# Feed-forwards with 512-column products over a rounded and a low half, summed at the drain

## The reference

```python
# four times, D = 1024, D_FF = 2816: ffn1 and ffn2 of two layers
x = x + 0.5 * swiglu(rmsnorm(x, ffn1_norm[layer]), ffn1_w_gu[layer], ffn1_w_down[layer])
def swiglu(h, w_gu, w_down):
    gate, up = jnp.split(h @ w_gu, 2, axis=-1)
    return (jax.nn.silu(gate) * up) @ w_down
...
# once, D_FF_2 = 4096: up, squared relu, down
```

## Time and profile before

| | before |
|---|---|
| median of 3 runs | 1651.73 us (1643.67 to 1655.06) |
| span of the profiled execution | 1644.7 us |
| TensorE matmuls busy | 1575.0 us, 96%, 15413 records |
| VectorE busy | 1066.6 us, 65% |
| ScalarE busy | 732.9 us, 45% |
| GpSimd busy | 69.7 us, 4% |
| DMA | 243.23 MB, 148 GB/s over the span |

### The profile page before, as it was taken

The page is one execution under the profiler, slowest core; times in us unless marked ns, Lnnn a source line. Parts: engine busy times, 40 slices in busy tenths (PEclk is TensorE's granted clock), DMA queues, the critical chain, the costliest instruction groups (busy, mean ns, idle before and its releaser), DMA issues.

```text
span 1644.7 us, 35602 instructions
## 1 busy us (share of the span) xinstructions
PE 1575.0 (96%) x15413; PEld 1514.6 (92%) x15413; DVE 1066.6 (65%) x1277; ACT 732.9 (45%) x814; POOL 69.7 (4%) x51
## 2 busy tenths in 40 slices
PE   7999999999999999999999999999979899999998
PEld 7999999888999999999979999988967778999997
DVE  5776497665866466663867665567676654877446
ACT  5433355443543354333555333455563323465333
POOL 2000000000100010000101000120000000100000
PEclk9999999998999999999999999999999998999999
DMA  8665544203565555655425655554300011555552
GB/s 268 186 197 194 191 154 163 70 3 103 180 195 189 204 180 179 188 189 186 155 81 168 187 180 192 186 175 131 105 2 2 3 53 52 180 182 202 186 199 77
DMA packets 155063, 243.23 MB, mean 148 GB/s; under 512 B 9283, under 2 KB 106174, under 8 KB 154814
## 3 DMA queue, kind: packets, MB, share of 16 engines
q1 hardware_dynamic: 154510, 240.63, 45.1%
q10 hardware_dynamic: 432, 0.79, 0.2%
HBM read 240.34 MB, written 1.05 MB: 147 GB/s over the span
## 4 chain that ended last, share of the span: by engine, by line
PE 87%; DVE 6%; ACT 3%; issue 1%; DMA 1%; POOL 0%; SPq 0%; ACTq 0%; DVEq 0%
PE dense_ps L2383 24%; PE dense_ps L2384 24%; PE dense_ps L2385 24%; PE mixer_ps L449 3%; PE dense_ps L449 2%; DVE w_lo L2753 1%; PE mixer_ps L1643 1%; PE mixer_ps L1081 1%; ACT ly_r L495 0%; PE mixer_ps L1072 0%; DVE xT L2871 0%; PE mixer_ps L1649 0%; DMA raw<-in_ffn_w_gu 0%; ACT score_b L1111 0%; ACT w_hi L2580 0%
## 5 line engine op out<-in xcount | busy, mean ns | idle before, releaser
L2753 DVE TENSOR_TENSOR w_lo<-raw,w_hi 128x2048 fp32r<-128x2048 f32 x225 | 523.2, 2336 | 241.7 <-ACT w_hi L2580 240.8
L2383 PE MATMUL dense_ps<-h_hi,w_hi 128*128 128x256 f32 x2368 | 667.6, 282 | 11.7 <-DVE h_lo L2828 8.1
L2384 PE MATMUL dense_ps<-h_lo,w_hi 128*128 128x256 f32 x2368 | 661.2, 279 | 0.0
L2385 PE MATMUL dense_ps<-h_hi,w_lo 128*128 128x256 f32 x2368 | 661.1, 279 | 0.0
L2580 ACT ACTIVATE w_hi<-raw 128x2048 fp32r<-128x2048 f32 x225 | 428.4, 1913 | 334.1 <-DMA raw<-in_ffn_w_down 116.7
L2383 PEld LDWEIGHTS dense_ps<-h_hi,w_hi 128*128 128x128 f32 x2368 | 450.8, 190 | 17.9 <-issue 17.3
L2384 PEld LDWEIGHTS dense_ps<-h_lo,w_hi 128*128 128x128 f32 x2368 | 447.4, 189 | 0.9 <-issue 0.5
L2385 PEld LDWEIGHTS dense_ps<-h_hi,w_lo 128*128 128x128 f32 x2368 | 447.4, 189 | 0.0
L2383 PE MATMUL dense_ps<-g_hi,w_hi 128*128 128x256 f32 x960 | 266.7, 278 | 0.0
L2384 PE MATMUL dense_ps<-g_lo,w_hi 128*128 128x256 f32 x960 | 266.7, 278 | 0.0
L2385 PE MATMUL dense_ps<-g_hi,w_lo 128*128 128x256 f32 x960 | 266.7, 278 | 0.0
(11 more groups left out here) (537 smaller groups left out, 1819.9 us busy)
## 6 DMA issues: line engine op xcount, KB each, us to landing
raw<-in_ffn_w_gu SPq DMA_DIRECT2D x176, 512.0 KB, 4.7
raw<-in_ffn_w_down SPq DMA_DIRECT2D x88, 512.0 KB, 4.2
raw<-in_w_ff SPq DMA_DIRECT2D x64, 512.0 KB, 4.2
raw<-in_w_in SPq DMA_DIRECT2D x36, 512.0 KB, 4.4
raw<-in_a_w_in SPq DMA_DIRECT2D x32, 512.0 KB, 4.4
raw<-in_a_w_out SPq DMA_DIRECT2D x8, 512.0 KB, 4.2
raw<-in_b_w_in SPq DMA_DIRECT2D x8, 512.0 KB, 4.2
raw<-in_b_w_out SPq DMA_DIRECT2D x8, 512.0 KB, 4.0
```

Of the source, the lines that this page charges most:

```text
L2383: pe.matmul(o, hi, mh, start=start, stop=False)
L2384: pe.matmul(o, hi, ml, start=False, stop=False)
L2385: return pe.matmul(o, lo, mh, start=False, stop=stop)
L2753: dve.tensor_tensor(w_lo[:, p % SLOTS, :], raw[:, p % SLOTS, :], w_hi[:, p % SLOTS, :].bitcast(F32), ALU.subtract).then_inc(lo_ready, 1)
```

## The change

It touches the feed-forwards only; the mixers keep `three`, their hi and low operands now lie in one tensor of two halves (`h_both`, `g_both` and so on).

- **The product** (`apart`): one matmul of 512 columns, w_hi on (h_hi, h_lo), fills one PSUM bank: hi·hi in its first 256 columns, hi·low in the other 256. A second matmul of 256 columns, w_lo on h_hi, adds to the first 256. Two matmuls and two weight loads stand for three and three. The sum of the two halves of the bank is left to the drain.
- **Up** (`run_ring`): a tile now takes a whole bank, so a piece is two tiles over all eight k (a piece of gate, then one of up), and four pairs of banks, D_ps and M_ps, are used in turn.
- **Drain of up**: after each piece ScalarE copies the second halves to SBUF (`side2`), VectorE adds the first halves to them (`summed`), then scales, multiplies as before; rounding to g_hi moves from VectorE to ScalarE. In ffn4 the relu no longer reads PSUM but the sum.
- **Down** (`run_half`): the output is computed in two halves of four tiles, each over all k, a half in four banks; the pieces are loaded to suit (512 columns of four k). The residual adds the two halves of each bank one after the other (`residual_apart`), the first half of the output midway through the down projection.
- **Start of a stage**: the first two pieces are taken for k 0 to 3 both, then for k 4 to 7.

```diff
-JOBS = [("gu0", "narrow", 11), ("down0", "wide", 11), ("a_in", "narrow", 8), ("a_out", "wide", 4),
-        ("gu1", "narrow", 11), ("down1", "wide", 11), ("gu2", "narrow", 11), ("down2", "wide", 11),
-        ("b_in", "narrow", 3), ("b_out", "wide", 4), ("gu3", "narrow", 11), ("down3", "wide", 11),
+JOBS = [("gu0", "ring", 22), ("down0", "half", 11), ("a_in", "narrow", 8), ("a_out", "wide", 4),
+        ("gu1", "ring", 22), ("down1", "half", 11), ("gu2", "ring", 22), ("down2", "half", 11),
+        ("b_in", "narrow", 3), ("b_out", "wide", 4), ("gu3", "ring", 22), ("down3", "half", 11),
         ("in2", "narrow", 9), ("up_attn", "wide", 2), ("up_rwkv", "wide", 2), ("out2", "wide", 4),
...
-            def three(o, hi, lo, mh, ml, start, stop):
-                pe.matmul(o, hi, mh, start=start, stop=False)
-                pe.matmul(o, hi, ml, start=False, stop=False)
-                return pe.matmul(o, lo, mh, start=False, stop=stop)
+            def three(o, hi, lo, both, start, stop):
+                pe.matmul(o, hi, both[:, 0, :], start=start, stop=False)
+                pe.matmul(o, hi, both[:, 1, :], start=False, stop=False)
+                return pe.matmul(o, lo, both[:, 0, :], start=False, stop=stop)
+            def apart(bank, hi, lo, both, start, stop):
+                pe.matmul(bank.rearrange("p (s t) -> p s t", s=2), hi, both, start=start, stop=False)
+                return pe.matmul(bank[:, 0:T], lo, both[:, 0, :], start=False, stop=stop)
+            def run_ring(job):
+                p0, f0, n = PIECE_OF[job], FILL_OF[job], COUNT_OF[job]
+                stage = stage_of[job]
+                h0 = h_before(stage)
+                groups = ring(stage)
+                def products(j, turn, ks, fresh=False):
+                    p = p0 + j
+                    ps, b = groups[j % 4]
+                    if ks[0] == 0:
+                        if j >= 4:
+                            pe.wait_ge(dense_drained, 2 + f0 + j - 4 + 1 + 4 * turn)
+                        pe.wait_ge(lo_ready, p + 1 + 4 * turn)
+                    for k in ks:
+                        if fresh and k % 2 == 0:
+                            pe.wait_ge(h_ready, h0 + k // 2 + 1)
+                        for i in range(2):
+                            w0 = 2 * P * k + P * i
+                            last = apart(ps[:, b + i, :], w_hi[:, p % SLOTS, w0:w0 + P], w_lo[:, p % SLOTS, w0:w0 + P],
+                                         h_both[:, :, k, :], start=k == 0, stop=k == KD - 1)
+                    if ks[-1] == KD - 1:
+                        last.then_inc(piece_used, 1)
...
+                    before = 2 + FILL_OF[BEFORE[stage]]
+                    pe.wait_ge(dense_drained, before + 1)
+                    products(0, 0, range(4), True)
+                    if stage == "ffn1":
+                        pe.wait_ge(dense_drained, before + 2)
+                    products(1, 0, range(4))
+                    products(0, 0, range(4, 8), True)
+                    products(1, 0, range(4, 8))
+                    pe.wait_ge(dense_drained, before + 2)
+                norm(stage)
+                products(2, 0, range(8))
+                pe.wait_ge(rstd_ready, NORM[stage] + 1)
+                products(3, 0, range(8))
...
+            def run_half(job, moving, ready, between=None, midway=lambda: None):
+                p0, f0, n = PIECE_OF[job], FILL_OF[job], COUNT_OF[job]
+                nk = 2 * n
+                def product(u, nt):
+                    e, k = divmod(u, nk)
+                    p = p0 + u // 4
+                    w0 = 512 * (u % 4) + P * nt
+                    return apart(half_banks(job, e)[:, nt, :], w_hi[:, p % SLOTS, w0:w0 + P],
+                                 w_lo[:, p % SLOTS, w0:w0 + P], moving[:, :, k, :], start=k == 0, stop=k == nk - 1)
+                for u in range(2 * nk - 4):
+                    e, k = divmod(u, nk)
+                    if k == 0:
+                        pe.wait_ge(dense_drained, 2 + f0 - 2 + 2 * e)
...
+                    if u % 4 == 0:
+                        pe.wait_ge(lo_ready, p0 + u // 4 + 1)
+                    if e == 0 and k % 2 == 0:
+                        pe.wait_ge(g_ready, ready + k // 2 + 1)
+                    for nt in range(4):
+                        last = product(u, nt)
+                    if u % 4 == 3:
+                        last.then_inc(piece_used, 1)
+                    elif u == nk - 1:
+                        last.then_inc(half_filled, 1)
...
+                pe.wait_ge(lo_ready, p0 + n)
+                for nt in range(4):
+                    for u in range(2 * nk - 4, 2 * nk):
+                        last = product(u, nt)
+                    if nt == 1:
+                        last.then_inc(half_filled, 1)
+                last.then_inc(piece_used, 1)
...
+                    def side(j, jq):
+                        ps, b = groups[jq]
+                        act.wait_ge(piece_used, p0 + j + 1)
+                        act.activation(side2[:, jq % 2, :, :], ps[:, b:b + 2, T:2 * T], ACT.Copy).then_inc(side_kept, 1)
+                    def gated_(c, q, t=0, at_=0, lead=False):
+                        side(2 * c, 2 * q)
+                        if not lead:
+                            split_hi(t, at_)
+                        act.wait_ge(gate_scaled, c0 + c + 1)
                         act.activation(act2[:, q, :, :], act2[:, q, :, :], ACT.Silu).then_inc(act_ready, 1)
+                        side(2 * c + 1, 2 * q + 1)
+                        split_hi(t, at_ + 1 - lead)
+                        act.wait_ge(g_full, c0 + c + 1)
+                        act.activation(g_hi[:, bass.ds(2 * c, 2), :], full2[:, q, :, :], ACT.Copy).then_inc(g_rounded, 1)
+                    def squared(j):
+                        side(j, j % 4)
+                        if j:
+                            splits(1)
+                        act.wait_ge(dense_drained, 2 + f0 + j + 1)
+                        act.activation(act2[:, j % 2, :, :], act2[:, j % 2, :, :], ACT.Relu).then_inc(gate_scaled, 1)
+                        act.wait_ge(gate_scaled, c0 + j + 1)
+                        act.activation(act2[:, j % 2, :, :], act2[:, j % 2, :, :], ACT.Square).then_inc(act_ready, 1)
+                        act.wait_ge(g_full, c0 + j + 1)
+                        act.activation(g_hi[:, 2 * j:2 * j + 2, :], full2[:, j % 2, :, :], ACT.Copy).then_inc(g_rounded, 1)
...
+            def residual_apart(job, scale):
+                f0, p0, n = FILL_OF[job], PIECE_OF[job], COUNT_OF[job]
+                after = next_stage(stage_of[job])
+                def added(e, a, b):
+                    acc, x_ = half_banks(job, e), xT[:, 4 * e + a:4 * e + b, :]
+                    for side in range(2):
+                        last = dve.scalar_tensor_tensor(out=x_, in0=acc[:, a:b, T * side:T * side + T], scalar=scale,
+                                                        in1=x_, op0=ALU.mult, op1=ALU.add)
+                        if not side:
+                            link(last)
+                    return last
+                splits_to(p0 + (n + 1) // 2 + 2)
+                wait_half(dve, job, 0)
+                added(0, 0, 4).then_inc(dense_drained, 1)
+                splits(1)
+                if after in LATE_SCALE:
+                    before_norm(after, 0)
+                splits_to(p0 + n + 2)
+                dve.wait_ge(half_filled, HALF_OF[job] + (2 if n % 2 else 1))
+                added(1, 0, 2)
+                wait_half(dve, job, 1)
+                added(1, 2, 4).then_inc(dense_drained, 1)
...
+                    def summed(j, jq, out_):
+                        ps, b = groups[jq]
+                        dve.wait_ge(side_kept, SIDE_OF[up] + j + 1)
+                        dve.tensor_tensor(out_, ps[:, b:b + 2, 0:T], side2[:, jq % 2, :, :],
+                                          ALU.add).then_inc(dense_drained, 1)
+                    def rest_of(c, q):
+                        dve.wait_ge(g_rounded, c0 + c + 1)
                         k = bass.ds(2 * c, 2)
-                        split_act(full2[:, q, :, :], g_hi[:, k, :], g_lo[:, k, :]).then_inc(g_ready, 1)
+                        dve.tensor_tensor(g_lo[:, k, :], full2[:, q, :, :], g_hi[:, k, :].bitcast(F32),
+                                          ALU.subtract).then_inc(g_ready, 1)
+                    def gated_(c, q, t=0, at_=0, lead=False):
+                        summed(2 * c, 2 * q, act2[:, q, :, :])
+                        if lead:
+                            dve.wait_ge(rstd_ready, NORM[s] + 1)
+                        else:
+                            rest_of(c - 1, 1 - q)
+                        dve.wait_ge(dense_drained, 2 + f0 + 2 * c + 1)
+                        dve.tensor_tensor(act2[:, q, :, :], act2[:, q, :, :], by_rms(2), ALU.mult).then_inc(gate_scaled, 1)
+                        if not lead:
+                            split_lo(t, at_)
```

(16 more changed lines are left out.)

409 lines of the change are left out of this document (234 added, 175 removed).

## The result

The changed kernel takes 1671.94 us in the median (1668.01 to 1673.00) against 1647.70 for the kernel before beside it: a ratio of 1.0177, 95% interval 1.0113 to 1.0241. In a later run it was 1670.59 against 1638.50, 1.0204 (1.0170 to 1.0238). So the change makes the kernel 1.8 to 2% slower. The forecast was 1655 us, some 3 us over the median of the kernel before, with the likeliest case between 1% less and 1% more; what came is a clear loss, near the upper end of the range. The profiled executions are 1644.7 and 1671.0 us long: 26.3 us are to be found.

What follows compares the result with a forecast made beforehand. TensorE, busy 96% of the span, was taken to bound the kernel. Terms of +2, +7.5 and -1.7 gave +7.8 on 1644.7, about 1652.5; 2.5 added for spread made 1655 us, range 1605 to 1675.

Steps and rivals of the forecast that it cites:

- Term 1: Feed-forwards: a pair takes 346 ns where triples took 340 or 353; +9.4 and -7.4 us, together +2 us.
- The load-bound rival: Feed-forwards: weight loads bind the triple, so the pair takes 328 ns and the kernel 1611 us; chance 0.25.
- Term 2: ff1: ScalarE and VectorE need 6.0 us a turn against TensorE's 5.5 a piece, so TensorE waits; +7.5 us.
- the wait of 0.8 us at the first piece: ff1, after four pieces: TensorE waits 0.8 us for the low part of piece 4.
- Term 3: Stage starts after a down projection: three TensorE waits for h_lo go, -1.7 us; other starts unchanged.
- starts that follow a mixer's output projection: Stages behind a mixer's output projection: TensorE waits as long as before, no change in time.
- mixer_a's start: Before mixer_a: last squares, norm and scaling stand in a row as before, so nothing gained or lost.
- At nothing: Gated drains, gated stage starts, PSUM, weight refills, down's loads and SyncE's issues: no cost expected.
- the slower cadence everywhere: All feed-forwards: matmuls of 239 and 118 ns, pair 357 ns, kernel 1678 or 1680 us; chance 0.15.

Runs made afterwards that it cites:

- the cut pair: The changed kernel with each 512-column matmul cut into two of 256 with a load each, everything else as changed: 1649.61 us, 1.0006 of the kernel before.

## Why the pair takes 353 ns

First a stream of TensorE alone, ScalarE and VectorE idle, with triples, pairs, and the wide matmul by itself, with its columns contiguous or in two runs.

```
triple: hi x h_hi, hi x h_lo, lo x h_hi  (256 columns each)
pair:   hi x (h_hi | h_lo)  (512 columns), lo x h_hi  (256)
```

> A stream of TensorE alone, with the other engines idle: 17 sections of 96 blocks, each of one form, with a pause between them. Sections: triple (three loads, three times 256 columns), pair (one load and 512 columns in two runs of 256 that lie 8 KB apart, one load and 256 columns), pair_near (the 512 columns contiguous), the 512 columns alone in both layouts, three times 256 columns into two halves of a bank, and 256 columns alone with the same and with new weights. The output is not the reference's: nothing but these matmuls is computed. Theory A (columns bind, 0.46 ns each, a load costs nothing): 256 columns 113 to 118 ns, 512 columns 227 to 235 ns, triple 340 to 353, pair 340 to 353, both forms alike. Theory B (a start of a record costs some ns beside the columns, so the wide one is cheaper than two): 512 alone 216 to 230 ns, pair 328 to 346, below the triple by 7 to 12 ns. Theory C (the two runs of columns cost): the contiguous pair is 5 to 13 ns below the pair. Theory D (the slow and the fast cadence come from traffic of the other engines): all triples here at 340; if the cadence is TensorE's own, triples at both 340 and 353 may be seen.

Steps from start to start, in the steady part of each section: triples 360 ns (three of 120), pairs 353 (347 in one section of four), with contiguous columns 353 as well, the wide matmul alone 227, 256 columns alone 120. So the two runs cost nothing, and the pair carries 7 ns over 227 + 120. On the load the stream says little: the sections of 256 columns with new and with the same weights both step by 120, but the trace has a load for each matmul in either. That the load is not what costs shows in the kernels, where three loads a block go at 340 and two at 353. But the triple of this stream is slower than the kernels' by 20 ns, and the order of pair and triple is turned round. Theory D, other engines' traffic, fell. The same in the order of a ring piece, with groups of wide ahead of narrow ones:

```
g16: 16 x (hi x (h_hi | h_lo)), then 16 x (lo x h_hi)
```

> TensorE alone again, now with the kernel's own order of a ring piece (two outputs by eight k, start flag on the first k alone), 96 blocks a section. Sections: triple into one half of a bank; pair; the cut pair; pairs grouped so that 2, 4, 8 or 16 wide matmuls stand before as many narrow ones; wide alone; 256 columns alone, new and same weights; then triple, pair, grouped and cut pair again behind 7, 8 or 9 unrounded matmuls. The output is not the reference's. The first such stream had triples at 361 ns, pairs at 355, wide alone 228, 256 columns alone 120. Theory A (a change between the two widths costs some 7 ns each time, since wide alone is 228 and not 235): groups of 16 at 228 + 120 = 348 or less, near 341 if the narrow ones fall to 113, groups of 2 halfway. Theory B (the step is set by something else, as the cadence of the stream): all groupings at 353 to 355. On the cadence: if the start flag on every block made 120 ns there, the triples come to 340 here; if it is what runs ahead of the section, only those behind unrounded matmuls do; if neither, all stay at 360.

Triples 360 again (behind unrounded matmuls too), pairs 347, groups of 2 at 348, of 4 at 351, of 8 at 349, of 16 at 348, counted over whole pieces. (The expectation for the third stream has 341 for the last; that is a misreading.) So in this stream grouping gains nothing over the fast pair. In the kernel, where the pair is at 353, the ring piece (the down projection likewise, by fours):

```diff
-                        pe.wait_ge(lo_ready, p + 1 + 4 * turn)
+                        pe.wait_ge(hi_ready, p + 1 + 4 * turn)
...
-                        for i in range(2):
-                            last = apart(ps[:, b + i, :], w_hi[...], w_lo[...], h_both[:, :, k, :], ...)
+                        for i in range(2):
+                            pe.matmul(ps[:, b + i, :].rearrange("p (s t) -> p s t", s=2), w_hi[...], h_both[:, :, k, :], ...)
+                    if ks[0] == 0:
+                        pe.wait_ge(lo_ready, p + 1 + 4 * turn)
+                    for k in ks:
+                        for i in range(2):
+                            last = pe.matmul(ps[:, b + i, 0:T], w_lo[...], h_both[:, 0, k, :], ...)
```

> The changed kernel with the order of the pairs changed and nothing else: in a ring piece the sixteen wide matmuls come first and the sixteen narrow ones behind them (four and four in a down projection), and the wait for the low part stands before the narrow ones, so the wide ones wait for the rounded weights alone. Theory A (alternating widths costs 7 to 13 ns a pair): 2624 pairs by 7 to 12 ns are 18 to 31 us, and 4 us of waits for low parts go too: 1640 to 1650 us. Theory B (353 ns is what the columns cost in this cadence): only the waits go, 5 to 6 us: 1665 to 1667 us.

1658.08 us against 1641.30, 1.0093 (1.0055 to 1.0132): between the theories. Steady pairs are at 346.7 ns in all feed-forwards but ff1, 6.6 ns less, 17 us by 2624. ff1 gives its 1.7 of them back: its turn of 5.88 us still binds, and TensorE idles 2.4 us at the start of ff2 now. The waits for w_lo at the starts became waits of 0.4 to 0.8 us for h_both. So in the kernel the order of the widths is worth 6.6 ns a pair. What sets the step, then? Busy neighbours or a loop of TensorE's program could:

> TensorE in the order of a ring piece, as in the second stream, with triples and pairs beside: nothing; ScalarE copying 512 columns again and again; VectorE subtracting 512 columns again and again; both; DMA loads; all three; then the same out of a loop of TensorE's program, and over one piece of weights alone. The output is not the reference's. The second stream, TensorE alone, had triples at 360 ns, pairs at 347 and pairs grouped by sixteen at 341; the kernels have triples at 340 or 353, pairs at 353, grouped ones at 347. Theory A (other engines' work sets the cadence): with some of them triples go to 340 or 353 and pairs to 353, and the section says which engine. Theory B (the loop or the fetch of instructions sets it): only the looped sections go to 340. Theory C (neither): all sections read 360 and 347, and what sets the cadence in the kernels stays open.

```
triple, pair, each with: nothing | ScalarE | VectorE | both | loads | all | a loop | a loop and all | one piece
```

All triples 360 ns, pairs 347 (three sections of ten) or 353 without any pattern: theory C. What was left was where the operands lie. w_hi starts at byte 16512 of a partition and w_lo at 49280, both multiples of 128, in the kernels as in the streams. h_both starts at 122688 in the kernels, 64 beyond a multiple of 128 (g_both too), and at 90240 in the streams, which is a multiple.

> TensorE alone in the order of a ring piece once more, to find what sets the step of a 256-column matmul: 120 ns in the three streams before, 113 or 118 in the kernels. The moving operand lies first where it lay in those streams, then at the place that h_both has in the kernel, and at places 32, 64, 512 and 1024 bytes off that; then with VectorE draining each filled pair of banks and TensorE waiting for it as in the ring; then with a moving operand of zeros. The output is not the reference's. Theory A (the operand's place): triples at 340 or 353 in some of the placed sections and not in others. Theory B (waits and drains between the pieces): only the drained sections change. Theory C (the data): only the zeros change. Theory D: all stay at 360 and 347 to 354, and the cause stays open.

```
h at byte 90240 | 122688 | 141152 | 159616 | 178496 | 199488: 0, 64, 96, 0, 64, 64 beyond a multiple of 128
```

Theory A. The windows of six sections (us; PE busy and count; granted clock), triple and pair by turns with the operand 64, 96 and 0 bytes beyond a multiple of 128:

```profile
110.00:138.00 28.00, 28.00 (x249) 1.00 0.00 1
142.00:172.00 30.00, 30.00 (x172) 1.00 0.00 1
176.00:206.00 30.00, 30.00 (x256) 1.00 0.00 1
212.00:242.00 30.00, 30.00 (x175) 1.00 0.00 1
245.00:275.00 30.00, 30.00 (x253) 1.00 0.00 1
280.00:310.00 30.00, 30.00 (x171) 1.00 0.00 1
```

A window counts one or two records that began ahead of it. At the kernels' place 28 us hold 247 matmuls, 113.3 ns each and 340 a triple, and 30 us 85 pairs, 353: the numbers of the two kernels, with no other engine at work. At 96 it is 355 and 347, at 0 360 and 353. (The last of the six places, at 64 as well, has 353 for both.) With VectorE draining the banks, or zeros for data, triples at 0 stayed at 360.

> TensorE alone: triples and pairs, 96 blocks a section, with the weights (one piece) at four places and the moving operand at four, each 0, 32, 64 or 96 bytes beyond a multiple of 2048. The output is not the reference's. Theory A (the place of the moving operand alone): the same four numbers come back for each place of the weights; the stream before had the operand at 0 modulo 128: triple 360, pair 347 or 354; at 64: triple 340 or 353, pair 354; at 96: triple 355, pair 347. Theory B (the distance between weights and operand): the numbers move along with the difference of the two. Theory C (neither, luck of a section's start): no pattern.

```
for each place of the weights (0, 32, 64, 96) and of h (0, 32, 64, 96): 96 triples, 96 pairs
```

Theory B, the distance between weights and operand. Ordered by distance (h less weights, modulo 128), four sections of each, ns per block in the steady part of the section:

| distance | triple | pair |
|---|---|---|
| 0 | 360, 360, 360, 360 | 353, 353, 353, 353 |
| 32 | 350, 350, 350, 352 | 347, 347, 347, 347 |
| 64 | 353, 353, 340, 353 | 353, 353, 353, 353 |
| 96 | 360, 355, 355, 355 | 350, 353, 353, 347 |

Two of the windows behind it, triples at distance 64 with the weights at 64 (340 ns) and at distance 32:

```profile
597.00:625.00 28.00, 28.00 (x250) 1.00 0.00 1
...
806.00:834.00 28.00, 28.00 (x242) 1.00 0.01 1
```

At 64 the triple has two steps, 340 and 353, the fast and the slow cadence of the earlier trace rows. Which one a section falls into, the streams don't say. Nor does the distance fix every pair: at 0 the first stream has 347 in one section of four, the second in all, the third in three of ten. Only 32 and 64 gave the same number each time for widths by turns, 347 and 353.

Now the same in the kernels: some unused bytes ahead of the operand, no instruction changed. Distance 32 for the changed kernel, with the changed kernel itself beside it:

```diff
+    fixed.at += 96
     h_at = fixed.at
```

> The changed kernel with 96 unused bytes ahead of h_both, so the moving operands lie 32 bytes beyond a multiple of 128, as far from the weights as in the four sections of the crossed stream where a pair took 347 ns (triples 350 to 353 there). If the distance sets the step in the kernel: pairs 347, 2624 by 6.7 ns are 17 us less than the changed kernel, triples of the mixers, some 980, at 350 for 346 are 4 us more: 1656 to 1660 us. If only the triple's step follows the place and the pair stays at 353: 1671 to 1676 us.

> The changed kernel itself, on the same chip as the one with the operand moved by 96 bytes: 1671 us within 4, 1.3 to 2.0% over the kernel before.

1657.66 us, 1.0123 (1.0089 to 1.0156), the changed kernel beside it 1670.59, 1.0204 (1.0170 to 1.0238): 12.9 us less, where 13 were worked out. In the profiled executions ffn0 to ffn3 gain 14.4 us and mixer_a loses 3.5; ffn4 gains only 1.6, since ff1 still takes 94.8 us: its pieces come every 5.88 us as before, where 16 pairs are 5.55. L2440 (the wide matmul of this file) has 462 records in 160 us, 346 ns a pair:

```profile
620.00:780.00 160.00, 160.00 (x462) 86.53 (x462) 1.00 0.58 192
900.00:1040.00 140.00, 140.00 (x405) 75.83 (x404) 1.00 0.58 188
```

Distance 96 and distance 0 (`fixed.at += 32` and `+= 64`):

> The changed kernel with 32 unused bytes ahead of h_both, so h_both, g_both and the mixers' operands behind them lie 32 bytes further; no instruction is changed. If the place sets the step as in the last stream (pair 347 for 354 ns), 2624 pairs by 6.7 ns are 17 us less, and the triples of the mixers, some 980, cost up to 15 ns more each for those that were at 340: 1655 to 1668 us. If the place does not matter in the kernel: 1671 us within 3.

> The changed kernel with 64 unused bytes ahead of h_both. If the place sets the step: pairs at 347 to 354, triples of the mixers at 360, so the time from 10 us under to 10 us over 1671 us. If not: 1671 us within 3.

1675.73 us, 1.0208 (1.0180 to 1.0235): pairs stay at 353, a miss of what I expected of 96, where the crossed stream has 347 once in four. And 1681.79 us, 1.0244 (1.0210 to 1.0278), 1 us over what I allowed for, with pairs at 353 as in the changed kernel; what is lost stands in the mixers, 7 us of it in mixer_a, where triples go at 360. Last the kernel before, with `fixed.at += 64` ahead of h_hi:

> The kernel before with 64 unused bytes ahead of h_hi and no instruction changed. If the place sets the step (triple 360 ns there, 340 or 353 now): 1568 triples by 20 ns, 1056 by 7 and some 980 of the mixers by 7 to 20 are 45 to 58 us more: 1695 to 1708 us. If not: 1650 us within 3.

1689.86 us against 1641.56, 1.0293 (1.0265 to 1.0320): 48 us for 64 unused bytes, as many more as expected (45 to 58), though from a lower start than the 1650 that I had counted from. The windows of its L2384 (the h_hi line):

```profile
620.00:780.00 160.00, 125.54 (x443) 84.98 (x443) 1.00 0.58 183
900.00:1040.00 140.00, 108.95 (x384) 73.77 (x384) 1.00 0.57 180
```

443 triples in 160 us are 361 ns, and from start to start it is 360 in all of them. So the place moves the step in both kernels. With the operand at distance 0 the change as it stands would have made the kernel a little faster (1681.79 against 1689.86, ratios 1.0244 and 1.0293 on one chip; the intervals just overlap).

## Why the prediction was wrong, point by point

**Term 1, the pair: the step that failed.** Counts, cover and the level of the fast and slow triple were right; the price of the pair was 346 ns and is 353, in all 2624: the term was +2 us and measured +20. The error has two parts. The wide matmul steps by 235 ns when a narrow one follows, not by 233, and the narrow one behind it by 118, not 113. I had priced the two apart, from neighbours of their own kind, and added the narrow one at the fast step. With neighbours of their own kind, sixteen wide and then sixteen narrow, the kernel takes just these 233 and 113. The runs show that the step belongs to the sequence of widths (347 in the kernel with the widths grouped) and to the place of the operands (347 at distance 32, in the stream and in the kernel). From the trace before nobody could read that. The error of method was to take the middle of 0.226, 0.233 and 0.239 and add 113, when the row at the top of the list was as good. That the 1568 fast triples lose and the 1056 slow ones gain was argued rightly: +9.4 and -7.4 were in truth some +20 and 0. Why the pair steps by 353 at this place is open.

The rule of the Trainium skill (TensorE: Matmul & The Clock Gate, Back-to-back issue gap), N / 2.4 + 2.5 ns from one matmul to the next without a budget for its load, would give 216 ns for 512 columns and 109 for 256. The streams disagree: 227 and 113 to 120 for rounded weights and operands. The same page has columns / 1.2 for a load (LDWEIGHTS), 107 ns at 128. That is less than the 109 of the matmul, so by these figures the triple would not have been bound by its loads, as the prediction says, and triple and pair would be 328 and 325 ns, an estimate from the page: no great gain either. The load-bound rival is refuted by the runs: the cut pair, with a third load, has 340, less than the pair's 353.

**Term 2, ff1: +7.5 forecast, 2.6 measured.** The turn was nearly right, 5.88 us for 6.0. TensorE's piece was not: 5.65 us for 5.5. The difference of two long times was to be 0.5 and is 0.24, and the wait of 0.8 us at the first piece did not come. (As written the term's parts, 0.8 and fourteen times 0.5, are 7.8 and not 7.5.) With blocks of 340 ns the term is 5.6 us (89.2 against 94.8); at the pair of the forecast, 347 ns at distance 32, it is twelve times 0.33, 4.0 us. The two terms had to be worked out together, at the same pair.

**Term 3, stage starts.** The waits of ffn2, mixer_b and the hybrid went, 1.7 us, as said. But "starts that follow a mixer's output projection: the same wait as now" was wrong by 3.5 us, and mixer_a's start "nothing" by 3.5 us. In the one I looked at the operation that TensorE waits for and not at the others in VectorE's queue: piece 1 is now wanted 2.8 us into the stage. In the other VectorE's chain was right, within 0.2 us; what I put at nothing was that half of the norm's matmuls leave the wait that they had filled, and that the rest then run at the lower clock.

**At nothing.** The gated drains, the banks and the DMA queue bound nothing. No wait for them stands in the gated stages of the changed kernel: 397 pairs in 140 us leave no room.

**Rivals.** The third, the slower cadence everywhere, which was to decide from 351 ns on, came nearest: every pair takes as long as the slow triple, though 353 and not 357. It had 0.15. In the earlier trace rows that cadence holds 40% of the blocks, so it deserved more. Its picture is only half right: at distance 0 the triple is at 360 and the pair still at 353, so the pair's step is its own.

Sum: +20.1 for the pair, +3.5 at the three starts, +3.5 before mixer_a, +1.6 at its first products, +2.6 in ff1, -1.7 at the other starts and -4.7 in the hybrid are 24.9 of the 26.3 us; 1.4 us, spread over the stages, stay unassigned. The hybrid's gain is not cadence: 225 of the 863 steps between the matmuls of in2's triples were fast, 351 before. It is the clock for the most part. Windows of the kernel before, then of the changed kernel at the same work (us; PE busy and count; granted clock):

```profile
1079.00:1083.00 4.00, 4.00 (x18) 0.57 0.67 245
1144.00:1148.00 4.00, 4.00 (x23) 0.57 0.00 0
```

```profile
1098.00:1102.00 4.00, 4.00 (x32) 1.00 0.63 240
1161.00:1165.00 4.00, 4.00 (x43) 1.00 0.14 22
```

Before, two stretches of in2 ran at 1.2 GHz, the first behind an idle time of 2.1 us, the second behind one of 2.3; they cost 1.5 us each. In the changed kernel the first idle time is 1.4 us, the second still 2.3, and the clock falls behind neither. Nothing in the change was meant to do that, and the other kernels have none, one or both of these stretches.

## What to carry to other kernels

A saved weight load or matmul was worth nothing here, where the columns and their step set the pace: price the new sequence as a whole, in a short stream with the operands at the places that they have in the kernel, before building around it. When a stream of TensorE is slower than its columns, look at the bytes of the operands in the partition before its order: a few unused bytes made one of these kernels 2.9% slower and the other 0.8% faster. And where a unit of work is wanted earlier, list everything that stands ahead of its producer in that engine's queue; where work is moved away, ask which wait it had filled.

## What the runs showed of the hardware

In these runs the step of a rounded matmul goes with the distance, modulo 128 bytes, of the moving operand from the weights in a partition: in triples, 256 columns take 120 ns at 0, 117 at 32, 113 or 118 at 64, and mostly 118 at 96, at a granted clock of 1.00 throughout. Why is open; that 64 has two steps with the same code and places is open too, and so is what makes a pair 347 or 353 at 0. Wide matmuls by themselves step by 227 ns (at distance 0), and narrow ones between them cost 7 ns a pair at most. Behind idle times of 1.8 and 2.8 us the granted clock was 0.56 and 0.57 for the next 3.5 us or so, with steps of 213 ns for 256 rounded columns; behind one of 2.3 us it was low in one kernel and not in the other; behind idle times of 1.0 to 1.4 us at the stage starts of the changed kernel it was 1.00:

```profile
427.90:433.00 5.10, 5.05 (x29) 1.00 0.00 0
893.70:899.00 5.30, 5.20 (x29) 1.00 0.01 3
```
